# Up-projections of a macaron decoder block by Strassen's scheme over pairs of tiles

## The chip, the cores and the metric

The kernel runs on the eight cores of one Trainium2 chip. Each core works on one of the eight sequences of the batch and exchanges nothing with the others. The metric is the device time in microseconds (us) of the slowest core.

## The reference

One decoder layer in float32 (batch 8, 4096 positions, width 1024, hidden width 2816). Three sub-layers follow one another, each behind an RMS norm that is scaled and shifted by vectors of the conditioning input `c`: a SwiGLU feed-forward network (FFN), a token mixer, and a second FFN. A last norm ends it.

```
mod = silu(c) @ w_mod + b_mod                       # nine vectors of 1024: shifts, scales, gates
h = ada_rmsnorm(x, g_ffn1, sh1, sc1)
gate, up = split(h @ w_in)                          # 1024 -> 2 x 2816
x = x + 0.5 * gt1 * ((silu(gate) * up) @ w_out)     # 2816 -> 1024
proj = ada_rmsnorm(x, g_mix, sh2, sc2) @ w_in_mix   # 1024 -> 2048
x = x + gt2 * concat(conv_group(proj), rglru_group(proj)) @ w_out_mix
... the second FFN with sh3, sc3, gt3, then the final ada_rmsnorm
```

The conv group is a gated unit, a causal depthwise convolution of width 31, a layer norm and a SiLU. The other group is a short convolution of width 4, two sigmoid gates by block-diagonal matrices, and a first-order recurrence along the sequence.

## The kernel before

A sequence is cut into eight tiles of T = 512 positions; a tile is held transposed, features on the partitions, as eight blocks of 128 x 512. All large products are bf16 matmuls of a 128 x 128 weight block with a 128 x 512 block, summed in one of eight PSUM banks (`mms`, L461). The weights come as slabs of 128 x 2048 bf16 (512 KB) into ten SBUF slots.

The first FFN takes tiles 0 to 5 in pairs and tiles 6 and 7 one by one; the second FFN takes all tiles one by one. In an FFN, for each of 22 chunks j of the hidden width (`ffn_in`), one slab holds the gate and up columns of the chunk: per tile eight matmuls make the gate, eight the up half, ACT takes the SiLU of the gate out of PSUM (`act`, L419), DVE multiplies it with the up half in PSUM (`tt`, L441). The down-projection (`ffn_out`) takes 22 matmuls for each of eight output blocks and adds the result to x (`stt`, L437). The float32 weights of the first FFN are cast on their first use by a DMA of the POOL queue and written back to HBM in bf16 by a DMA of the SP queue; later tiles read that copy. `w2o` is treated so too. `win`, `dcw`, `wout` (mixer) and `w2i` (second FFN) are cast from HBM to HBM by the POOL queue while the first FFN runs (`prep`). The conditioning vectors (`mods`, L536) are 88 multiplications of DVE over 128 x 1024 slabs of `w_mod`.

The mixer works on pairs of tiles: `mix_in` per tile (norm, projections, the recurrence), `mix_conv` per pair, `mix_out` per tile; then the tile goes straight on into the second FFN, its x staying in SBUF. All DMAs stand in the queues of SP (plain) and POOL (casts, most stores), all plain DMA issues on L468.

The order of all this isn't the order in the code. `Program.add` records every operation with a duration in a table of the author, a priority and its buffers; `schedule` is a list scheduler, which for each engine takes the next operation by readiness and priority, gives it a buffer of its pool, and so fixes what stands in each engine's queue; slabs are loaded in the order in which their users came out of a first pass. `emit` turns the dependencies into semaphore waits. The engines then run their queues in order. Float32 blocks come from a pool of 40 buffers (`p2`), bf16 blocks from a pool of 62 (`p1`).

## Time and profile before

| what | value |
|---|---|
| runs | 2373.24 us median of 3 (2370.82 to 2373.36) |
| profiled execution, span of its slowest core | 2371.6 us, spans of the eight cores 2357.1 to 2371.6 |
| PE busy | 2258.1 us, 95% of the span |
| DVE, ACT, POOL busy | 1164.3, 1000.2, 197.9 us |
| DMA | 503.88 MB, 212 GB/s in the mean |

The span runs from the first to the last instruction of the core. The page gives no other time of the profiled execution, so the sum of the prediction is made against this span; the median of the runs is 1.6 us above it. PE's busy time counts from the start of a matmul to its modelled end, so the step from one matmul to the next is read from counts over a long window and not from the mean duration. A window's row gives each engine's busy time and count in that stretch.

### The profile page before, as it was taken

The page shows a single profiled execution, that of the slowest core. Times are in us where ns is not written, and L with a number is a line of the kernel's source. Part 1 is how long each engine was busy: PE and PEld are TensorE (multiplying, and loading weights), DVE is VectorE, ACT ScalarE, POOL GpSimd, SP SyncE. Part 2 cuts the span into 40 slices and gives each one's busy share as a digit, 9 for nine tenths or more (in the row PEclk, how much of TensorE's full clock was granted, in tenths as well). Part 3 has the DMA queues.
Part 4 walks back from the last instruction along what each step waited for, and adds up shares of the span by engine and source line. Part 5 has one row for each costly group of instructions (what it writes and reads, how often), then busy time and mean ns, then how long its engine had stood idle before and what let it go on. Part 6 is the DMA issues. An engine that isn't in the chain of part 4 may idle for free.

```text
span 2371.6 us, 34311 instructions; the slowest of 8 cores (2357.1 to 2371.6 us)
## 1 busy us (share of the span) xinstructions
PE 2258.1 (95%) x10692; PEld 1068.2 (45%) x10898; DVE 1164.3 (49%) x1898; ACT 1000.2 (42%) x1445; POOL 197.9 (8%) x374
## 2 busy tenths in 40 slices
PE   2999999999999998999998899999999999999997
PEld 0444444444444453444454344454444454444446
DVE  6325241413143796644685425687426786232423
ACT  2314011401122974304975415886416876231422
POOL 0001100110011003000003001003001003000000
PEclk9999999999999999999999999999999999999998
DMA  9899877797779989999579746667557577455455
GB/s 250 188 258 223 249 227 163 165 188 191 145 178 218 228 225 293 298 290 299 165 202 260 226 158 225 195 209 246 194 165 227 187 237 258 154 191 178 176 188 178
DMA packets 184642, 503.88 MB, mean 212 GB/s; under 512 B 53856, under 2 KB 56032, under 8 KB 183776
## 3 DMA queue, kind: packets, MB, share of 16 engines
q1 hardware_dynamic: 161088, 414.87, 55.2%
q0 software_dynamic: 23376, 86.79, 19.0%
q8 instruction: 92, 1.51, 0.3%
q14 instruction: 86, 0.70, 0.1%
HBM read 482.45 MB, written 88.60 MB: 241 GB/s over the span
## 4 chain that ended last, share of the span: by engine, by line
PE 82%; DMA 6%; DVE 5%; SPq 3%; issue 2%; ACT 1%; DVEq 0%; ACTq 0%; POOLq 0%
PE ps L461 82%; SPq L468 3%; DVE sb_c L437 2%; DMA sb_slab<-w1i 2%; DMA sb_slab<-wmod 1%; DVE sb_c L441 1%; DMA sb_slab<-b_w2i 1%; DMA b_w2o<-sb_slab 1%; DMA sb_slab<-w2o 1%; DVE sb_h L441 1%; ACT sb_c L419 0%; DMA sb_h<-yseq 0%; DVE sb_c L447 0%; ACT L419 0%; DVE sb_c L823 0%
## 5 line engine op out<-in xcount | busy, mean ns | idle before, releaser
L461 PE MATMUL ps<-sb_h,sb_slab 128*128 128x512 bf16 (+1 forms) x9960 | 2172.6, 377 | 63.9 <-ACT sb_h L419 28.2
L461 PEld LDWEIGHTS ps<-sb_h,sb_slab 128*128 128x128 bf16 x10160 | 996.8, 98 | 1222.2 <-issue 77.6
L441 DVE TENSOR_TENSOR sb_h<-ps,sb_c 128x512 bf16<-128x512 f32 x352 | 242.6, 691 | 657.3 <-PE ps L461 558.6
L419 ACT ACTIVATE sb_c<-ps 128x512 f32<-128x512 f32 (+1 forms) x392 | 230.7, 592 | 754.3 <-PE ps L461 731.7
L441 DVE TENSOR_TENSOR sb_c<-sb_c 128x512 f32<-128x512 f32 (+1 forms) x524 | 336.3, 674 | 78.4 <-ACT sb_c L419 73.0
L419 ACT ACTIVATE sb_c<-sb_c 128x512 f32<-128x512 f32 (+1 forms) x324 | 190.2, 610 | 264.5 <-DVE sb_c L437 241.2
L419 ACT ACT_TABLE_LOAD x167 | 214.3, 1283 | 175.2 <-PE ps L461 163.3
L437 DVE SCALAR_TENSOR_TENSOR sb_c<-ps,sb_gth,sb_c 128x512 f32<-128x512 f32 (+1 forms) x136 | 97.8, 719 | 287.1 <-PE ps L461 278.5
L536 DVE SCALAR_TENSOR_TENSOR sb_slab<-sb_slab,sb_crow 128x1024 f32<-128x1024 f32 x88 | 107.4, 1221 | 36.7 <-DMA sb_slab<-wmod 33.5
L419 ACT ACTIVATE sb_h<-sb_c,sb_modv,sb_gs 128x512 bf16<-128x512 f32 x138 | 102.8, 802 | 34.4 <-DVE sb_modv L441 24.1
L905 POOL DMA_DIRECT2D yseq<-sb_h x128 | 67.8, 537 | 154.3 <-ACT sb_h L419 152.5
L468 POOL DMA_DIRECT2D y<-sb_c x56 | 30.5, 546 | 599.0 <-ACT sb_c L419 321.0
L437 DVE SCALAR_TENSOR_TENSOR sb_c<-sb_ux,sb_vecs,sb_c 128x512 f32<-128x512 f32 x96 | 72.1, 751 | 11.1 <-DVE sb_c L437 0.9
L461 PE MATMUL ps<-sb_ub,sb_slab 128*128 128x256 bf16 x576 | 65.7, 273 | 1.5 <-ACT sb_c L419 1.0
L441 DVE TENSOR_TENSOR sb_h<-sb_c 128x512 bf16<-128x512 f32 (+1 forms) x82 | 55.5, 677 | 21.8 <-ACT sb_c L419 16.7
L468 POOL DMA_DIRECT2D xmid<-sb_c x64 | 35.3, 552 | 321.0 <-DVE sb_c L437 315.1
L461 PEld LDWEIGHTS ps<-sb_ub,sb_slab 128*128 128x128 bf16 x576 | 56.0, 98 | 10.8 <-issue 2.2
L437 DVE SCALAR_TENSOR_TENSOR sb_c<-ps,sb_modv,sb_c 128x512 f32<-128x512 f32 x64 | 47.4, 748 | 22.6 <-PE ps L461 18.6
L419 ACT ACTIVATE sb_c<-sb_c,sb_lam 128x512 f32<-128x512 f32 x64 | 50.7, 807 | 1.5
L419 ACT ACTIVATE sb_c<-ps,sb_cst 128x512 f32<-128x512 f32 (+1 forms) x33 | 22.3, 675 | 67.0 <-PE ps L461 64.8
L419 ACT ACTIVATE sb_ux<-ps 128x512 f32<-128x512 f32 x32 | 35.1, 1109 | 28.2 <-PE ps L461 27.6
L461 PE MATMUL ps<-sb_h,sb_ones 128*128 128x512 bf16 (+1 forms) x62 | 23.2, 382 | 24.6 <-DVE sb_h L441 24.6
(56 smaller groups left out, 537.9 us busy)
## 6 DMA issues: line engine op xcount, KB each, us to landing
sb_slab<-b_w2i SPq DMA_DIRECT2D x176, 512.0 KB, 4.0
sb_slab<-b_w2o SPq DMA_DIRECT2D x96, 512.0 KB, 3.6
sb_slab<-wmod SPq DMA_DIRECT2D x88, 512.0 KB, 9.8
sb_slab<-b_w1i SPq DMA_DIRECT2D x88, 512.0 KB, 6.2
sb_c<-xmid SPq DMA_DIRECT2D x128, 256.0 KB, 7.2
sb_slab<-b_win SPq DMA_DIRECT2D x64, 512.0 KB, 4.4
sb_slab<-b_w1o SPq DMA_DIRECT2D x48, 512.0 KB, 6.0
sb_slab<-b_dcw SPq DMA_DIRECT2D x36, 512.0 KB, 4.5
```

Source lines behind the costliest of these rows:

```text
L419: return A("ACT", dur, lambda: (lambda o, i: (lambda h: [h.activation(out=o, in_=i, func=func, bias=bias, scale=scale)]))(out(), in_()), r ...
L437: return A("DVE", dur, lambda: (lambda o, a, b: (lambda h: [h.scalar_tensor_tensor(out=o, in0=a, scalar=scalar, in1=b, op0=op0, op1=op1)]) ...
L441: return A("DVE", dur, lambda: (lambda o, a, b: (lambda h: [h.tensor_tensor(out=o, in0=a, in1=b, op=op)]))(out(), in0(), in1()), reads, wr ...
L461: return [h.matmul(o, lhsT=l, rhs=r, start=(first and i == 0), stop=(last and i == n - 1)) for i, (l, r) in enumerate(pr)]
L468: lambda: (lambda o, i: (lambda h: [h.dma_start(out=o, in_=i)]))(out(), in_()),
L536: return lambda h: [h.scalar_tensor_tensor(out=w, in0=w, scalar=1.0, in1=crow.ap, op0=ALU.mult, op1=ALU.mult, accum_out=o)]
L905: return lambda h: [h.dma_start(out=yc_d[rows[q]:rows[q] + 64, :].rearrange("(g c) n -> c g n", c=32), in_=src[32 * q:32 * q + 32]) for q ...
```

## The change

The up-projection of a chunk for a pair of tiles is a product of a 2 x 2 block matrix of weights (gate and up columns by two halves of the 1024 features) with a 2 x 2 block matrix of activations (two halves of the features by two tiles). The change computes it with seven block products in place of eight, by Winograd's form of Strassen's scheme. A block product is four matmuls of 128 x 512.

- **Weights.** The first pair of each FFN computes plainly (`plain_in`), with slabs cast on use, for `w2i` now too. On each such slab DVE makes four sums of weight blocks in bf16 (`slab_sums`), and SP writes three blocks and the four sums to HBM (`keep_in`), 896 KB for a chunk. The other three pairs read these as two slabs per chunk.
- **Activations.** For a pair DVE makes four sums of blocks of the normed input in bf16 (`hb_sums`).
- **A chunk** (`quick_in`): seven products into three PSUM banks x, y and z. ACT copies three partial results to SBUF, DVE adds three further ones from PSUM to those, ACT takes one SiLU over 128 x 1024, DVE multiplies twice. Bank x is used by four products in turn, each of which adds to what stands there after ACT or DVE has read it.
- **Order.** Both FFNs go by pairs, `ffn(s)` with s = 0 to 3 for the first and 4 to 7 for the second; s = 0 and 4 are plain. The mixers of the pairs 0 to 3 are laid into s = 2, 3, 4 and 5 by the table `MIX`. `mix_out` stores x to HBM, and an FFN loads x twice, for the norm and again for the down-projection. The down-projection stays plain (`QOUT` is off).
- **Memory.** One pool (`gp`, 156 units of 1 KB per partition, a buffer being one, two or four adjoining units) takes the place of `p1` and `p2`; slots for slabs go from ten to eight. Loads and stores of x are of 512 KB. Squares, norm scalings and their sums work on 128 x 1024. The modulation's rows after the first sixteen go through `gp`.
- **Last tile.** Its down-projection isn't split into halves of 256 columns any more.

```diff
-NSLOT = 10
-N_P2 = 40
-N_P1 = 62
+NSLOT = 8
...
+QOUT = False
+NG = 156
...
+MIX = [[(2, 1), (2, 6), (2, 12), (2, 16), (2, 19)],
+       [(3, 1), (3, 6), (3, 12), (3, 16), (3, 19)],
+       [(4, 1), (4, 6), (4, 12), (4, 16), (4, 19)],
+       [(5, 1), (5, 6), (5, 12), (5, 16), (5, 19)]]
...
+        def hb_sums(B, prio):
+            row = lambda i: B[i].q[0].ap.bitcast(BF16)
+            for o, a, b in ((T1, T1, B11), (T2, B22, T1), (T3, T2, B11), (T4, B21, T2)):
+                op = sub16(lambda o=o: row(o), lambda a=a: row(a), lambda b=b: row(b), B[a].q + B[b].q, B[o].q, 4 * T, prio=prio)
+            return op
...
+            sub16(out(0), a21, a22, [slab], [q], n, prio=prio, op=ALU.add, after=after)
+            sub16(out(1), out(0), a11, [slab], [q], n, prio=prio)
+            sub16(out(2), a11, a21, [slab], [q], n, prio=prio)
+            sub16(out(3), a12, out(1), [slab], [q], n, prio=prio)
...
+        def keep_in(nm, j, slab, prio, after=()):
...
+            q = slab_sums(slab, 4, prio, after)
+            wb = dmas("SP", [(d[:, 0:1536], lambda: slab.ap[:, 0:1536])], D_SLAB * 0.75, lambda: wb_sems[slab.slot], [slab], [scr_i[nm][j][0]], prio=prio)
+            dmas("SP", [(d[:, 1536:3584], lambda: q.ap.bitcast(BF16))], D_SLAB, slot_sem(q), [q], [scr_i[nm][j][1]], prio=prio)
...
+            prod(x_, "A11", B11, True, True)
+            copy(ga, x_, dd)
+            prod(z_, "S1", T1, True, True)
+            copy(lambda: c.ap, z_, c)
+            prod(x_, "S2", T2, False, True)
+            copy(gb, x_, dd)
+            prod(y_, "A12", B21, True, True)
+            plus(ga, y_, dd)
+            prod(z_, "S4", B22, False, True)
+            plus(gb, z_, dd)
+            prod(x_, "S3", T3, False, True)
+            plus(lambda: c.ap, x_, c)
+            act(lambda: dd.ap, lambda: dd.ap, AF.Silu, [], [dd], dur=act_us(2 * T), tset=(SILU,), prio=250)
+            last = prod(x_, "A22", T4, False, True)
+            (ha, ha_ap), (hb_, hb_ap) = H[2 * hf][k], H[2 * hf + 1][k]
+            tt(ha_ap, lambda: x_.ap, ga, ALU.mult, [x_, dd], [ha], prio=250)
+            tt(hb_ap, lambda: c.ap, gb, ALU.mult, [c, dd], [hb_], prio=250)
...
+                    slab = cast_slab(wi, j, sync=sync, after=casts[-1:], lat=DMA_LAT if s == 0 and j < 10 else 6.0)
...
+                    op = plain_in(B, H, slab, j, split=(s == 0 and j == 0))
+                    wb = keep_in(wi, j, slab, P.prio + 20, after=(op,) if s == 0 and j < 6 else ())
...
+                    sa = slab_of(w_scr[wi][128 * j:128 * j + 128, 0:2048], scr_i[wi][j], name=f"{wi}{j}a")
+                    sb_ = slab_of(w_scr[wi][128 * j:128 * j + 128, 2048:3584], scr_i[wi][j][1:], cols=1536, name=f"{wi}{j}b")
+                    op = quick_in(B, H, sa, sb_, j, start)
```

How the queues read, at three places. The first is PE in the up-projection of a full FFN step, before (groups of eight matmuls, one bank each, with the semaphores a group waits for) and now, where slab1 holds A11, S1, A12 and A22 of one chunk and slab7 its S2, S3 and S4; slab0 belongs to the chunk before, slab3 to the next.

```order
L461 MATMUL ps<-sb_h,sb_slab 128x512 [waits s_slabSP6,s_dve]
L461 MATMUL ps<-sb_h,sb_slab 128x512 x7
L461 MATMUL ps<-sb_h,sb_slab 128x512 [waits s_dve]
L461 MATMUL ps<-sb_h,sb_slab 128x512 x7
L461 MATMUL ps<-sb_h,sb_slab 128x512 [waits s_dve]
```

```order
L558 MATMUL ps<-sb_gp,sb_slab0 128x512 [waits s_dve]
L558 MATMUL ps<-sb_gp,sb_slab0 128x512 x3
L558 MATMUL ps<-sb_gp,sb_slab7 128x512 [waits s_slabSP7,s_act]
L558 MATMUL ps<-sb_gp,sb_slab7 128x512 x3
L558 MATMUL ps<-sb_gp,sb_slab1 128x512 x4
L558 MATMUL ps<-sb_gp,sb_slab7 128x512 [waits s_act]
L558 MATMUL ps<-sb_gp,sb_slab7 128x512 x3
L558 MATMUL ps<-sb_gp,sb_slab7 128x512 [waits s_act]
L558 MATMUL ps<-sb_gp,sb_slab7 128x512 x3
L558 MATMUL ps<-sb_gp,sb_slab3 128x512 [waits s_slabSP3,s_dve]
```

Before, a group waits for a free bank and a slab; now a group of four waits for ACT or DVE to have read the same chunk's earlier product. Between two products of one chunk that hang on one another stand two other products: A22 of the chunk before behind S1, A12 and S4 behind S2, and A11 and S1 of the next chunk behind S3.

The second place is the queue of POOL around the cast of the second FFN's up weights, before (HBM to HBM, during the first FFN) and now (into slabs, in `ffn(4)`); `useq` and `yseq` are stores of the mixers.

```order
L468 DMA xmid<-sb_c 128x512
L468 DMA b_w2i<-w2i 16x16384
L468 DMA useq<-sb_h 128x512 x4
L468 DMA b_w2i<-w2i 16x16384 x4
L468 DMA useq<-sb_h 128x512 x4
L468 DMA b_w2i<-w2i 16x16384 x2
```

```order
L565 DMA sb_slab<-w2i 128x2048 x5
L565 DMA xmid<-sb_gp 128x1024
L565 DMA sb_slab<-w2i 128x2048 x2
L1193 DMA yseq<-sb_gp 32x2x256 x8
L565 DMA xmid<-sb_gp 128x1024
L1193 DMA yseq<-sb_gp 32x2x256 x24
L565 DMA xmid<-sb_gp 128x1024 x8
L565 DMA sb_slab<-w2i 128x2048
L565 DMA useq<-sb_gp 128x512
L565 DMA sb_slab<-w2i 128x2048
```

Seven of the 22 casts now stand ahead of the mixer's stores of pair 1, the other fifteen behind them. The third place is the queue of SP in the same stretch of the changed kernel: the writing of kept weights (`b_w2i`), between the loads of the mixer.

```order
L573 DMA b_w2i<-sb_slab 128x1536 x3
L565 DMA sb_gp<-xmid 128x1024 x4
L573 DMA b_w2i<-sb_slab 128x1536
L565 DMA sb_slab<-b_wout 128x2048 x2
L573 DMA b_w2i<-sb_gp 128x2048
L565 DMA sb_gp<-xmid 128x1024 x4
L573 DMA b_w2i<-sb_gp 128x2048
```

A write of sums waits for DVE; the loads of `xmid` and `wout` behind it are what `mix_out` needs.

## Rows read from the trace of the kernel before

**Rows 1.** Page, part 1: busy us of each engine (share) and instructions.
```profile
PE 2258.1 (95%) x10692; PEld 1068.2 (45%) x10898; DVE 1164.3 (49%) x1898; ACT 1000.2 (42%) x1445; POOL 197.9 (8%) x374
```

**Rows 2.** Windows, core 0: length; PE, PEld, DVE, ACT, POOL busy; PEclk, DMA share, GB/s.
```profile
0.00:60.00 60.00, 14.37 (x51) 5.85 (x53) 38.23 (x82) 16.96 (x23) 3.54 (x10) 1.00 0.95 250
100.00:700.00 600.00, 597.05 (x2726) 272.00 (x2781) 202.63 (x314) 132.06 (x212) 49.14 (x94) 1.00 0.85 201
780.00:1380.00 600.00, 564.03 (x2661) 267.44 (x2712) 377.25 (x620) 325.53 (x455) 63.27 (x118) 0.97 0.84 247
840.00:900.00 60.00, 59.59 (x348) 34.30 (x352) 55.14 (x96) 45.54 (x68) 2.12 (x5) 1.00 0.86 229
960.00:1080.00 120.00, 119.42 (x546) 54.41 (x556) 67.33 (x114) 21.26 (x33) 4.34 (x8) 1.00 0.90 295
1200.00:1260.00 60.00, 56.58 (x320) 32.15 (x326) 52.08 (x88) 43.21 (x65) 5.84 (x11) 0.97 0.87 217
1260.00:1380.00 120.00, 103.16 (x449) 45.85 (x458) 51.27 (x79) 51.77 (x76) 21.32 (x40) 0.93 0.79 236
1560.00:1620.00 60.00, 57.80 (x337) 33.13 (x340) 52.68 (x87) 46.25 (x76) 0.52 (x1) 1.00 0.74 237
1920.00:1980.00 60.00, 57.66 (x338) 33.12 (x341) 51.17 (x80) 43.08 (x76) 13.18 (x25) 1.00 0.71 237
2316.00:2336.00 20.00, 20.00 (x185) 17.84 (x183) 6.55 (x14) 2.92 (x7) 0.00 (x0) 1.00 0.83 268
2340.00:2372.00 32.00, 15.30 (x139) 13.31 (x137) 12.28 (x32) 11.64 (x25) 0.00 (x0) 0.77 0.30 103
```

**Rows 3.** Groups by line and shape: count | busy us, mean ns | idle before.
```profile
L441 DVE TENSOR_TENSOR sb_c<-sb_c 128x512 f32<-128x512 f32 x500 | 327.2, 686 | 72.1 <-ACT sb_c L419 66.8 <-DVE sb_c L431 0.2 <-DVE sb_c L441 0.2
L441 DVE TENSOR_TENSOR sb_h<-ps,sb_c 128x512 bf16<-128x512 f32 x352 | 242.6, 691 | 657.3 <-PE ps L461 558.6 <-ACT sb_c L419 88.4 <-remote 8.3
L419 ACT ACTIVATE sb_c<-ps 128x512 f32<-128x512 f32 x384 | 228.0, 597 | 743.9 <-PE ps L461 722.0 <-remote 14.0 <-DVE sb_slab L536 6.0
...
L536 DVE SCALAR_TENSOR_TENSOR sb_slab<-sb_slab,sb_crow 128x1024 f32<-128x1024 f32 x88 | 107.4, 1221 | 36.7 <-DMA sb_slab<-wmod 33.5
...
L437 DVE SCALAR_TENSOR_TENSOR sb_c<-ps,sb_gth,sb_c 128x512 f32<-128x512 f32 x120 | 90.0, 750 | 271.1 <-PE ps L461 262.4 <-remote 8.4
...
L419 ACT ACTIVATE sb_crow<-sb_crow 128x1024 f32<-128x1024 f32 x1 | 1.1, 1057 | 0.0
```

**Rows 4.** DMA queues of the whole run, page part 3: packets, MB, share of 16 engines.
```profile
q1 hardware_dynamic: 161088, 414.87, 55.2%
q0 software_dynamic: 23376, 86.79, 19.0%
```

**Rows 5.** DMA of the window 60 to 240 us: queues, then one issue group.
```profile
q0 software_dynamic: 4284, 15.52, 54.1%
q1 hardware_dynamic: 8102, 24.59, 42.2%
...
sb_slab<-b_w1i SPq DMA_DIRECT2D x1, 512.0 KB, 26.8
```

**Rows 6.** Chain that ended last, one piece: start, us, what.
```profile
1304.09 19.23 DMA sb_slab<-b_w2i
```

**Rows 7.** Timeline of the last stretch: start, us, engine, operation, [idle before].
```profile
2355.03 0.48 DVE L437 SCALAR_TENSOR_TENSOR sb_c<-ps,sb_gth,sb_c 128x256 f32<-128x256 f32 x1 [0.81 <-PE ps L461]
2355.60 0.42 ACT L419 ACTIVATE sb_c<-sb_c 128x256 f32<-128x256 f32 x1 [1.99 <-DVE sb_c L437]
2356.19 0.42 DVE L441 TENSOR_TENSOR sb_h<-sb_c 128x256 bf16<-128x256 f32 x1 [0.68 <-ACT sb_c L419]
...
2356.76 0.27 PE L461 MATMUL ps<-sb_h,sb_ones 128*128 128x256 bf16 x1 [1.73 <-DVE sb_h L441]
2357.13 0.47 ACT L419 ACTIVATE sb_c<-ps,sb_cst 128x256 f32<-128x256 f32 x1 [1.11 <-PE ps L461]
...
2361.42 0.41 DVE L427 TENSOR_SCALAR sb_c<-sb_c,sb_gs,sb_modv 128x256 f32<-128x256 f32 x1
```

More of the change, by code:

```diff
@@ L136, in reset, with spots, earliest, take @@
     def reset(self):
-        self.res = [Res() for _ in self.aps]
-        self.free = list(range(self.n))
+        self.res = [Res() for _ in range(self.n)]
+        self.busy = [False] * self.n
+        self.best = {}
+    def spots(self, size):
+        for s in range(0, self.n - size + 1, size):
+            run = range(s, s + size)
+            if not any(self.busy[i] for i in run):
+                yield max(self.res[i].free_t for i in run), s
+    def earliest(self, size):
+        if size not in self.best:
+            self.best[size] = min((t for t, _ in self.spots(size)), default=None)
+        return self.best[size]
+    def take(self, size, now):
+        def cost(spot):
+            t, s = spot
+            quad = range(s - s % 4, min(self.n, s - s % 4 + 4))
+            return (max(t - now, 0.0), -sum(self.busy[i] for i in quad), t, s)
+        _, s = min(self.spots(size), key=cost)
+        for i in range(s, s + size):
+            self.busy[i] = True
+        self.best = {}
+        return s
+    def give(self, s, size):
+        for i in range(s, s + size):
+            self.busy[i] = False
+        self.best = {}
 class VB:
-    def __init__(self, pool=None, ap=None, name=""):
+    def __init__(self, pool=None, ap=None, name="", size=1, spare=0):
         self.pool = pool
@@ L267, in start_of @@
                     continue
-                fr = b.pool.free
-                if not fr:
+                free_t = b.pool.earliest(b.size)
+                if free_t is None or b.pool.n - sum(b.pool.busy) < b.size + b.spare:
                     return None
-                t = max(t, min(b.pool.res[s].free_t for s in fr))
+                t = max(t, free_t)
         return t
@@ L451, in cp, with mms @@
             return A("DVE", dur, lambda: (lambda o, i: (lambda h: [h.tensor_copy(out=o, in_=i)]))(out(), in_()), reads, writes)
-        def mms(bank, pairs, reads, first=True, last=True, cols=512, sub=None, prio=None, after=()):
+        def mms(bank, pairs, reads, first=True, last=True, cols=512, sub=None, prio=None, after=(), more=False):
             n = len(pairs)
@@ L460, in g @@
                 def g(h):
-                    return [h.matmul(o, lhsT=l, rhs=r, start=(first and i == 0), stop=(last and i == n - 1))
+                    return [h.matmul(o, lhsT=l, rhs=r, start=(first and i == 0), stop=(last and i == n - 1), skip_group_check=more)
                             for i, (l, r) in enumerate(pr)]
@@ new lines, in slab_sums @@
+        def slab_sums(slab, nk, prio, after=()):
+            n = 128 * nk
+            q = new(4, "sums")
+            blk = lambda i: (lambda: slab.ap[:, n * i:n * i + n])
+            out = lambda i: (lambda: q.ap.bitcast(BF16)[:, n * i:n * i + n])
+            a11, a12, a22, a21 = (blk(i) for i in range(4))
+            sub16(out(0), a21, a22, [slab], [q], n, prio=prio, op=ALU.add, after=after)
+            sub16(out(1), out(0), a11, [slab], [q], n, prio=prio)
+            sub16(out(2), a11, a21, [slab], [q], n, prio=prio)
+            sub16(out(3), a12, out(1), [slab], [q], n, prio=prio)
+            return q
@@ new lines, in build_program, with mixer @@
+        yrs = {}
+        def mixer(s, ev, pr, gate_op):
+            P.prio = 500 + 100 * s - 40
+            gate_op = (gate_op, ends[s - 1])
+            if ev < 2:
+                yrs[pr, ev] = mix_in(2 * pr + ev, gate_op, P.prio - 5)
+            elif ev == 2:
+                yrs[pr, 2] = mix_conv(pr, gate_op)
+            else:
+                mix_out(2 * pr + ev - 3, yrs[pr, ev - 3], gate_op)
+            if s in out_x:
+                for o in out_x[s][XG:]:
+                    o.after.append(P.last)
@@ L996, in emit_cb @@
             fn = (op.fn if op.on == op.eng else op.alt[2])()
[L997 to L998 removed]
+            rs = [r for b in op.reads for r in b.res]
+            ws = [r for b in op.writes for r in b.res]
             e = engs[op.on]
```

806 lines of the change are left out of this document (483 added, 323 removed).

## The prediction

> **What bounds the kernel now.** The busy times say PE: 2258.1 of 2371.6 us, with DVE and ACT at half and less [rows 1]. The windows say how [rows 2]. From 100 to 700 us PE loads 2781 weight blocks in 600 us, 0.2158 us for a 512-column matmul, at full clock (PEclk 1.00); only fewer matmuls shorten such a stretch. In 2316 to 2336 it is 20 us for 183 to 185 matmuls of 256 columns, 0.1087 us each. The built program has 9934 of 512 and 964 of 256 columns, so 2143.8 + 104.8 = 2248.6 us of matmuls; the other 10 us of PE's busy time are stretches at half clock and ends of chains.
>
> PE is idle for 113.5 us: 45.6 before the first products (60 less 14.37), 16.7 behind the last (32 less 15.30), 36.0 between 780 and 1380, 15 elsewhere [rows 2]. Part of the middle is DMA: the chain of waits has a load of `b_w2i` there that took 19.2 us [rows 6], and 1260 to 1380 lost 16.8 us [rows 2], where the twelve casts of `w2o` stand. Where DVE is densest, 51 to 55 us of 60, PE idles for 0.4, 3.4, 2.2 and 2.3 us, in the mean 2.1 us in 60 [rows 2].
>
> **The matmuls removed.** Three pairs in each of two FFNs have 22 chunks: 132 chunks, each with 28 matmuls for 32, 528 less. The last tile's 352 halves become 176 whole ones. The new program has 9584 and 608: 2068.2 + 66.1 = 2134.3 us. All of it lies on the path, as PE is the bound: **-114.3 us**. The rest of the sum asks how much of that is given back.
>
> **The chain inside a chunk.** PE needs 28 x 0.2158 = 6.04 us for a chunk, DVE 5 x 0.691 = 3.46, ACT 3 x 0.597 + 1.057 = 2.85 [rows 3]. What is new is that PE waits for readers of its own results. The hops are in the last stretch [rows 7]: PE to ACT 0.10 (2356.76 + 0.27 to 2357.13), DVE to ACT 0.09, ACT to DVE 0.17, DVE to PE 0.15. A result stands 0.16 us after the next matmul can start (0.27 for 256 columns against a step of 0.11). Behind A11 the copy takes 0.16 + 0.10 + 0.60 + 0.15 = 1.01 us, and two other products (1.73 us) stand between, as the order shows: 0.7 us to spare. S2 to S3 has the same; S3 to A22, over DVE, takes 0.16 + 0.10 + 0.69 + 0.15 = 1.10, with 0.6 to spare. So a step without mixer (s = 1, 6, 7) should run without gaps; I take 2 us each for s = 6 and 7.
>
> **DVE in the mixer steps.** PE's time in such a step is 968 matmuls of the FFN and 400 whole and 160 half ones of the mixer, 208.9 + 86.3 + 17.4 = 312 us. DVE's 1164.3 us [rows 1] less modulation (107.4), the FFN's multiplications (242.6) and its adds (90.0) [rows 3] leave 724 us for mixers and 24 norms of tiles: 181 us a pair, and 162 without the final norm (2 x 14 x 0.686). So s = 2 and 3 have 22 x 3.46 + 16 x 0.75 + 24 x 1.22 (modulation) + 162 + the four sums of activations. These, and the 176 sums of weights in s = 0 and 4, are bf16 with bf16, which no row here shows. From the float rows (512 elements 0.686, 1024 elements 1.221) 2048 would take 0.686 + 3 x 0.535 = 2.29 us as the upper end; half of it is the lower. I take the upper, as the nearest rows are two-tensor operations too. Then DVE has 289 us of 312, 93%, for whole steps; s = 5, without modulation but with a final norm, 89%; s = 4, with 60 us of weight sums, 284 of 332. Those are the shares of today's densest windows, so I take their 2.1 us in 60: 11 us each in s = 2 and 3, 9 in s = 5. The Trainium skill, "VectorE: DVE Perf Modes", section on the perf-mode tier table, says that a `tensor_tensor` of 16-bit operands in SBUF runs at twice the float rate, 1224 ns for 2048 elements; by it s = 2 falls to 284 us and the sum by less than 1 us.
>
> **DMA.** The plain queue took 55.2% of 2371.6 us for 414.87 MB, 3.16 us a MB [rows 4]. With many casts, from 60 to 240, POOL's queue took 54.1% of 180 us for 15.52 MB, 6.27 us a MB [rows 5]. Each chunk now reads 0.92 MB where a pair read 0.52, x moves more often, and kept weights add 20.2 MB of writes to each plain step. By step, from the sizes in the program, MB of casts and of the rest: s = 0, 17.3 and 47.5, 259 us in 273; s = 1, 11.0 and 47.0, 217 in 209; s = 2 and 3, 85.3 plain, 270 in 312; s = 4, 17.3 and 72.7, 338 in 332; s = 5, 230 in 312; s = 6 and 7, 122 in 209. So s = 1 and s = 4 ask for a little more than there is. For a cover speaks that 295 GB/s (960 to 1080) left PE 119.4 of 120 us [rows 2], and that eight slots, four chunks of two slabs, are 24 us of lead; against it, that a load of `b_w1i` among the casts landed after 26.8 us [rows 5]. I take 5 us for s = 0, 10 for s = 1, and 20 for s = 4, where POOL's queue holds fifteen casts behind the mixer's stores, and SP's holds `mix_out`'s loads behind writes that wait for DVE. The ends: nothing at all (first rival), and all of the excess (second).
>
> **Start and end.** The first slabs, the modulation and the first tile's norm are the same work; 0, between -2 and +5 (two slots fewer). At the end the last block of x goes through wider operations: add 0.75, square 1.06, add 1.22, two of 0.69, two of ACT's 0.6, four scalings of 1.22, one last of 0.6, with PE and the hops some 12.5 us from the last product, where about 7 passed before (just ahead of 2355.03, to 2361.42 + 0.41) [rows 7]. The last store is of 512 KB in place of 128, 2 us more at the rate above with its landing. **+8 us**, at least 3 (scalings beside other work), at most 12.
>
> **The sum.** Idle inside the run: 5 + 10 + 11 + 11 + 20 + 9 + 4 = 70 us against 113.5 - 45.6 - 16.7 = 51.2, so +18.8. 2371.6 - 114.3 + 18.8 + 8 = 2284.1 us of span; the median of the runs shown is 1.6 above the span, so **2286 us**. 0.2% of the time, 4.7 us, is about what a measurement of this kernel can tell from no change.
>
> **Rivals.** *All cover holds* (14%): the planner spreads DMA better than my rows, the stalls of 780 to 1380 go, DVE's gaps are filled with other products. Inside idle is 15 us: 2371.6 - 114.3 - 36 + 8 + 1.6 = 2231; with half of that gain 2249.
>
> *DMA becomes the bound* (17%): each of 21 casts in s = 1 and 34 in s = 4 costs what each of the twelve of `w2o` cost, 16.8 / 12 = 1.4 us [rows 2], 29 and 48 us. Inside idle is 5 + 29 + 22 + 48 + 9 + 4 = 117: 2371.6 - 114.3 + 66 + 8 + 1.6 = 2333, and up to 2346 with half clock behind the stalls (PEclk below 1 in that window). For it speaks the 26.8 us landing; against it, that both queues fill 96% of 60 to 240 us [rows 5] with PE at work. The Trainium skill, "DMA: Bandwidth & Descriptors", section on queues, rings and completion order, says that each DMA engine takes the queues it has work for in turn, packet by packet, so that slab loads get no precedence over casts; by that rule this rival is what s = 1 and 4 do, and the landing of 26.8 us agrees.
>
> *The chain inside a chunk costs more than the product it saves* (10%, the other side): ACT or DVE takes a mixer's or a norm's operation ahead of a copy, and PE stands. It decides from (114.3 - 8 - 18.8) / 132 = 0.66 us a chunk, the spare time of one hop. With one 1.22 us operation ahead on two hops of each chunk, 2 x (1.22 - 0.6) = 1.24 us, 164 us in all: 2450. Against it: without a mixer both engines are half free.
>
> *No change* (4%): the prices just cancel, 2369 to 2378. That the matmuls aren't removed is excluded by the counts of the built programs.
>
> **Chances and range.** The forecast's own range, 2262 to 2310 by the bounds above, has 55%. Faster by over 0.2%: 55 + 14 + 17 = 86%; same 4%; slower 10%. The range 2238 to 2346 leaves out half of the first rival and the last two, some 20%.
>
> **What would show it.** Right: weight loads at 0.2158 us through s = 1, 6 and 7; in s = 2, 3 and 5 idle PE of 2 us in 60, released by DVE and ACT; DVE near 70% of the span; the idle of s = 1 and 4 released by slabs. Wrong: PE released by ACT's copies or DVE's adds all through s = 6 and 7 (third rival); tens of us behind slabs in s = 1 or 4 (second); full clock lost over long stretches.

## The result and the profile after

| | before | after |
|---|---|---|
| median | 2372.03 us of 4 runs | 2345.48 us of 4 runs (2343.05 to 2350.86) |
| after to before | | 0.9895, 95% interval 0.9879 to 0.9911 |
| profiled execution, slowest core | span 2371.6 us | span 2349.3 us (core 2), time 2350.86 us |

The change makes the kernel 1.05% faster; 3.6% was forecast, and 2345 us stands at the upper end of the range. Executions in which a whole die ran slower, or that took over 1.5% more than the kernel's fastest, are left out of every ratio and interval.

Page, part 1, of the changed kernel; it answers to [rows 1].

```profile
PE 2175.2 (93%) x10192; PEld 997.4 (42%) x10192; DVE 1487.4 (63%) x2277; ACT 1189.6 (51%) x1602; POOL 181.1 (8%) x342
```

PE has the 10192 matmuls that were counted. The next rows are the windows of the changed kernel, core 2, one for each step (columns as in [rows 2]). A step goes from its first product to that of the next one; the built program says how many products stand between. The first row is the start, the last one what lies behind the last matmul.

```profile
0.00:48.90 48.90, 1.17 (x2) 0.22 (x3) 34.08 (x75) 12.39 (x15) 2.70 (x8) 1.00 0.93 267
48.90:312.10 263.20, 239.25 (x1062) 105.33 (x1063) 115.89 (x199) 67.32 (x90) 19.61 (x37) 0.97 0.90 222
312.10:566.60 254.50, 220.19 (x973) 95.79 (x972) 126.22 (x182) 86.20 (x117) 14.82 (x29) 0.94 0.97 227
566.60:864.60 298.00, 289.58 (x1401) 136.41 (x1400) 230.61 (x357) 197.68 (x265) 9.18 (x17) 0.99 0.78 243
864.60:1191.40 326.80, 318.11 (x1529) 148.46 (x1528) 246.59 (x387) 201.66 (x278) 33.79 (x63) 0.99 0.84 257
1191.40:1545.20 353.80, 340.42 (x1620) 159.01 (x1619) 225.56 (x368) 191.36 (x251) 40.75 (x76) 0.98 0.91 251
1545.20:1868.00 322.80, 314.07 (x1516) 147.67 (x1515) 238.52 (x344) 222.52 (x297) 32.38 (x60) 1.00 0.70 222
1868.00:2112.90 244.90, 241.29 (x1124) 109.28 (x1123) 150.88 (x208) 113.29 (x162) 23.50 (x44) 1.00 0.66 215
2112.90:2331.60 218.70, 210.54 (x975) 95.14 (x973) 113.46 (x156) 91.29 (x124) 4.35 (x8) 0.99 0.46 152
2331.60:2349.30 17.70, 0.58 (x1) 0.07 (x1) 5.56 (x6) 5.87 (x8) 0.00 (x0) 0.50 0.39 157
```

Take from a step's length its matmuls at the full rate (0.2158 us, 0.1087 for half ones), and what is left is its **loss**. For s = 0 that is 263.2 - 1062 x 0.2158 = 34.0 us; the other steps follow in the same way (s = 2, 3 and 4 have 152 half matmuls each, s = 5 has 135, s = 6 has 17).

| step | forecast | measured loss, core 2 |
|---|---|---|
| s = 0 | 5 | 34 |
| s = 1 | 10 | 44.5 |
| s = 2, 3 | 11 each | 12, 13 |
| s = 4 | 20 | 20.5 |
| s = 5 | 9 | 10 |
| s = 6, 7 | 2 each | 4, 0 up to its last product |

Six steps lost about as much as was forecast. Two didn't, by 29 and 34.5 us, and that is nearly all of the miss: 2349.3 against 2284.1 us of span. The other cores show the same (s = 0 29.5 to 36.9, s = 1 38.2 to 44.8 on the six cores whose matmul records are complete). Of the two losses 24.0 and 34.3 us are idle PE (lengths less busy times); the forecast's 5 and 10 are idle time too. The other 10 us of each are matmuls slower than the full rate (busy times less the full-rate times), at a granted clock of 0.97 and 0.94 in the mean of the step.

Where PE stood, from the timeline of PE in s = 0 and 1 (start, us, operation, [idle before and releaser]):

```profile
87.02 31.93 PE L558 MATMUL ps<-sb_gp,sb_slab 128*128 128x512 bf16 x136 [7.19 <-ACT sb_gp L516]
...
194.08 8.87 PE L558 MATMUL ps<-sb_gp,sb_slab 128*128 128x512 bf16 x32 [6.61 <-DVE sb_gp L538]
207.40 37.24 PE L558 MATMUL ps<-sb_gp,sb_slab 128*128 128x512 bf16 x164 [4.45 <-DVE sb_gp L538]
...
395.32 20.16 PE L558 MATMUL ps<-sb_gp,sb_slab 128*128 128x512 bf16 x84 [8.93 <-DMA sb_slab<-b_w1i]
...
450.19 4.49 PE L558 MATMUL ps<-sb_gp,sb_slab 128*128 128x512 bf16 x12 [5.71 <-DMA sb_slab<-b_w1i]
462.51 5.15 PE L558 MATMUL ps<-sb_gp,sb_slab 128*128 128x512 bf16 x12 [7.83 <-DMA sb_slab<-b_w1i]
```

In s = 0 the first wait is for the second tile's norm. The next two are named after DVE, and DVE's own timeline says why DVE was late:

```profile
192.10 1.23 DVE L653 SCALAR_TENSOR_TENSOR sb_gp<-sb_gp 128x1024 f32<-128x1024 f32 x1 [11.46 <-DMA sb_gp<-wmod]
205.42 1.23 DVE L653 SCALAR_TENSOR_TENSOR sb_gp<-sb_gp 128x1024 f32<-128x1024 f32 x1 [10.89 <-DMA sb_gp<-wmod]
```

Two rows of the modulation stood at the head of DVE's queue before their loads had landed, and the chunks' operations behind them waited too. In s = 1 the waits are slabs of kept weights. The DMA view of 360 to 480 us has the reason (queues, then an issue group with KB and median landing):

```profile
q1 hardware_dynamic: 5717, 19.25, 56.9%
q0 software_dynamic: 414, 6.82, 42.2%
...
sb_slab<-b_w1i SPq DMA_DIRECT2D x11, 512.0 KB, 22.3
```

99% of the engines' time is taken: 42.2% by POOL's queue, nearly all of it casts, at 0.422 x 120 / 6.82 = 7.4 us a MB, and 56.9% by SP's. A slab of kept weights takes 22.3 us to land (median). Ahead of that s = 0 has a hole. The windows of 60 to 120 us, and POOL's next cast:

```profile
60.00:80.00 20.00, 19.82 (x92) 8.82 (x90) 9.98 (x18) 10.34 (x13) 1.06 (x2) 1.00 0.75 168
80.00:100.00 20.00, 12.98 (x49) 5.43 (x50) 11.18 (x23) 8.11 (x12) 0.53 (x1) 0.83 0.23 59
100.00:120.00 20.00, 18.95 (x88) 8.42 (x86) 10.14 (x24) 3.58 (x6) 1.59 (x3) 1.00 1.03 223
```

```profile
95.99 0.53 POOL L565 DMA_DIRECT2D sb_slab<-w1i  x1 [29.07 <-DVE sb_gp L538]
```

All eight slots are held until the second tile's norm is there, so the casts pause for 29 us and DMA runs at 23%; from 100 to 280 us it is full.

### The profile page after: what moved, and what is told of

The parts are those of the page before. It is cut to its first block, busy times and chain, and to the rows that moved or that the text cites. A ratio compares the mean times of both kernels' runs of the same rounds, so it can differ in the third digit from the quotient of the medians.

```text
span 2349.3 us, 34252 instructions; the slowest of 8 cores (2328.6 to 2349.3 us)
## 1 busy us (share of the span) xinstructions
PE 2175.2 (93%) x10192; PEld 997.4 (42%) x10192; DVE 1487.4 (63%) x2277; ACT 1189.6 (51%) x1602; POOL 181.1 (8%) x342
## 4 chain that ended last, share of the span: by engine, by line
PE 75%; DMA 12%; DVE 3%; ACT 3%; SPq 3%; issue 3%; DVEq 0%; ACTq 0%; POOLq 0%
PE ps L558 75%; DMA sb_slab<-b_w1i 3%; ACT sb_gp L516 2%; DVE sb_gp L538 2%; SPq L565 2%; DMA sb_gp<-x 2%; DMA b_w1i<-sb_slab 1%; DMA sb_gp<-wmod 1%; DMA sb_slab<-b_wout 1%; DMA sb_slab<-w1i 1%; DMA sb_slab<-b_dcw 1%; DMA sb_gp<-xmid 1%; SPq L573 1%; ACT L516 1%; DMA sb_slab<-wmod 1%
## 5 line engine op out<-in xcount | busy, mean ns | idle before, releaser
L558 PE MATMUL ps<-sb_gp,sb_slab 128*128 128x512 bf16 x9456 | 2090.1, 382 | 105.9 <-DVE sb_gp L538 27.6
L558 PEld LDWEIGHTS ps<-sb_gp,sb_slab 128*128 128x128 bf16 x9456 | 926.9, 98 | 1246.4 <-issue 165.2
L538 DVE TENSOR_TENSOR sb_gp<-ps,sb_gp 128x512 f32<-128x512 f32 (+1 forms) x616 | 419.9, 689 | 296.6 <-PE ps L558 181.5
L538 DVE TENSOR_TENSOR sb_gp<-sb_gp 128x512 bf16<-128x512 f32 (+3 forms) x596 | 518.7, 894 | 120.5 <-ACT sb_gp L516 109.7
L516 ACT ACTIVATE sb_gp<-ps 128x512 f32<-128x512 f32 (+1 forms) x556 | 321.3, 589 | 526.3 <-PE ps L558 496.5
L516 ACT ACTIVATE sb_gp<-sb_gp 128x1024 f32<-128x1024 f32 (+2 forms) x342 | 314.7, 927 | 355.4 <-DVE sb_gp L538 149.3
L534 DVE SCALAR_TENSOR_TENSOR sb_gp<-ps,sb_gth,sb_gp 128x512 f32<-128x512 f32 x128 | 95.6, 748 | 180.8 <-PE ps L558 179.2
L516 ACT ACTIVATE sb_gp<-sb_gp,sb_modv,sb_gs 128x512 bf16<-128x512 f32 (+1 forms) x203 | 157.6, 807 | 64.9 <-DVE sb_gp L538 37.2
L653 DVE SCALAR_TENSOR_TENSOR sb_gp<-sb_gp 128x1024 f32<-128x1024 f32 x72 | 87.6, 1216 | 35.7 <-DMA sb_gp<-wmod 35.6
L534 DVE SCALAR_TENSOR_TENSOR sb_gp<-sb_ux,sb_vecs,sb_gp 128x512 f32<-128x512 f32 x96 | 72.1, 751 | 9.6
L538 DVE TENSOR_TENSOR sb_gp<-sb_slab 128x512 bf16<-128x512 bf16 x88 | 36.9, 421 | 27.3 <-DMA sb_slab<-w1i 23.3
```

What stands on the lines that cost most here:

```text
L516: return A("ACT", dur, lambda: (lambda o, i: (lambda h: [h.activation(out=o, in_=i, func=func, bias=bias, scale=scale)]))(out(), in_()), r ...
L534: return A("DVE", dur, lambda: (lambda o, a, b: (lambda h: [h.scalar_tensor_tensor(out=o, in0=a, scalar=scalar, in1=b, op0=op0, op1=op1)]) ...
L538: return A("DVE", dur, lambda: (lambda o, a, b: (lambda h: [h.tensor_tensor(out=o, in0=a, in1=b, op=op)]))(out(), in0(), in1()), reads, wr ...
L558: return [h.matmul(o, lhsT=l, rhs=r, start=(first and i == 0), stop=(last and i == n - 1), skip_group_check=more) for i, (l, r) in enumera ...
L653: return lambda h: [h.scalar_tensor_tensor(out=a, in0=a, scalar=1.0, in1=c, op0=ALU.mult, op1=ALU.mult, accum_out=o)]
```

## The experiments

Losses are worked out as above, on the cores with complete records, and ranges are over those cores. Where one pair of cores ran at a granted clock of 0.81 in a step (last section), that pair is left out of that step. In the changed kernel s = 0 lost 33 us in the mean of the cores. All diffs are against the changed kernel unless it says otherwise; as the planner orders the whole program anew for each edit, steps that an edit doesn't name can change too.

**Second tile's x early.**

```diff
-                        wait_for(x1_loads[j // 2], casts[max(0, j - 3)])
+                        wait_for(x1_loads[j // 2], casts[0])
```

> The loads of the second tile's x in s = 0 wait only for the first cast. In the changed kernel s = 0 takes 263 us for 229 us of matmuls (34 lost) and s = 1 takes 254 us for 210 (45 lost). Theory of order (eight slots, all held until the second tile's norm is there, and casts that stop meanwhile): the pause of POOL's casts from 66 to 96 us shrinks to about 15 us, s = 0 loses 15 us or less, the time falls by about 20 us. Theory of bytes (DMA is full, whatever the order): only the idle DMA time of 75 to 96 us can come back, s = 0 loses 20 to 30 us, s = 1 still about 45, the time falls by 5 to 12 us. Theory of the chain inside a chunk: no change.

s = 0 lost 17.8 to 31.2 us (mean 25), s = 1 36.3 to 42.2; ratio to before 0.9895 (0.9819 to 0.9971), that of the changed kernel. Some 8 us came back in s = 0, which is what the theory of bytes gave. The theory of order wasn't put to a full test: the pause of the casts fell to 21 us and not to 15 (POOL, core 7).

```profile
85.56 0.53 POOL L565 DMA_DIRECT2D sb_slab<-w1i  x1 [21.18 <-DVE sb_gp L538]
```

**Fewer bytes in s = 0.** `keep_in` returns for `w1i` behind one write; the later steps read columns 0 to 1536 for the second slab. The return stands behind `slab_sums`, so DVE still makes the sums (116.20 us and 200 operations in s = 0 on core 5, where the changed kernel's core 2 has 115.89 and 199): only the writing is left out, not the computing.

```diff
+            if nm == "w1i":
+                return dmas("SP", [(d[:, 0:2048], lambda: slab.ap[:, 0:2048])], D_SLAB, lambda: wb_sems[slab.slot], [slab], scr_i[nm][j], prio=prio)
```

> The writing of the sums of w1i and their computing in s = 0 are left out: SP writes one block of 128 x 2048 for a chunk in place of 128 x 1536 and 128 x 2048, 8.65 MB less, and the later steps read as many bytes as now, plain blocks in the place of sums. Theory of bytes: at 3.28 us a MB of the plain queue (46.6% of 180 us for 25.59 MB) 28 us of DMA go, s = 0 loses about 8 us in place of 34, s = 1 still about 45; the time falls by about 25 us. Theory of order: the slots come free at the same points, s = 0 loses at least 25 us. Theory of the chain: no change in s = 0 either, as it is plain.

s = 0 lost 24.2 to 30.5 us (mean 27); ratio 0.9865 (0.9806 to 0.9924). 8.65 MB were worth 6 us and not 28: bytes alone don't make this loss.

**No preparing casts.**

```diff
-            jobs = [(a, q) for a in batch if isinstance(a, int) for q in range(8)] + [j for j in prep if j[0] in batch]
+            jobs = [(a, q) for a in batch if isinstance(a, int) for q in range(8)]
...
-            return slab_of(dr(w_scr[nm], r), [scr[nm][r]], prio=prio, after=after, name=f"{nm}{r}")
+            return slab_of(dr(w_scr["w1i"], r)[:, 0:2048], scr_i["w1i"][r], prio=prio, after=after, name=f"{nm}{r}")
```

> The 21 casts of win, dcw and wout in s = 1 are left out, and the mixers read kept blocks of w1i in their place, as many bytes. Theory of bytes: 11 MB at 7.4 us a MB (42.2% of 120 us for 6.82 MB), some 80 us of DMA, are gone from s = 1, which then loses under 12 us in place of 45; s = 0 as before at 34; the time falls by 35 us or more. Theory of order (x loads and slabs stand in one queue, gated by the planner): s = 1 still loses 25 us or more. Theory of the chain inside a chunk: s = 1 still loses about 40 us, as its chunks are the same.

This kernel leaves out the mixers' weights and reads other blocks in their place. The window of s = 1, core 5 of this run:

```profile
309.60:519.30 209.70, 209.70 (x973) 95.06 (x972) 126.24 (x182) 85.27 (x117) 4.25 (x8) 1.00 0.68 225
```

PE is busy for 209.70 of 209.70 us. The whole loss of s = 1 goes with 21 casts (0 to 0.9 us on four cores), so each cost 2 us in the mean, and the chunks of Strassen's scheme run without a gap when their slabs are there. s = 0 kept 32.0 to 35.9. Ratio 0.9714 (0.9638 to 0.9790).

**The first FFN plain.**

```diff
+            if nm == "w1i":
+                return dmas("SP", [(d[:, 0:2048], lambda: slab.ap[:, 0:2048])], D_SLAB, lambda: wb_sems[slab.slot], [slab], scr_i[nm][j], prio=prio)
...
+                elif not second:
+                    slab = slab_of(w_scr[wi][128 * j:128 * j + 128, 0:2048], scr_i[wi][j], name=f"{wi}{j}a")
+                    op = plain_in(B, H, slab, j, split=False)
```

> The first FFN computes plainly in all four pairs, with its plain weights kept (512 KB written and read a chunk); Strassen's scheme is left in the second FFN. 264 matmuls come back, 57 us. Theory of bytes: s = 0 loses about 8 us in place of 34 and s = 1 about 20 us of 229 in place of 45 of 210, so that 2349 + 57 - 26 - 25 or about 2350 us come out: the scheme in the first FFN brings next to nothing. Theory of order: s = 0 and 1 lose as much as now, and the time is 2349 + 57 = 2406 us. Theory of the chain: s = 1 loses nothing, s = 0 as now, 2349 + 57 - 45 = 2361.

The windows of s = 0 and 1, core 5:

```profile
47.40:305.40 258.00, 238.44 (x1062) 105.51 (x1063) 77.46 (x108) 66.10 (x89) 19.57 (x37) 0.96 0.79 194
305.40:556.50 251.10, 232.94 (x1061) 104.51 (x1060) 78.79 (x113) 50.81 (x72) 14.78 (x29) 0.96 0.81 197
```

The slowest core had a span of 2395.6 us, so the scheme in the first FFN is worth some 46 us of its 57. None of the three expectations (2350, 2406 and 2361 us) is met; that of order is nearest. In s = 1 the scheme brings nothing: with 88 matmuls more this step takes 240 to 254 us (mean 246), where it takes 248 to 254.5 (mean 251) with the scheme. There DMA is busy for 97% of it, here for 81%. The gain comes from s = 2 and 3: 685.9 us together here (core 5), 624.8 with the scheme (core 2), though part of that is mixers' work which the plan laid into another step. And s = 0, without any sums, still lost 25.0 to 28.9.

**The casts of dcw one step later.**

```diff
-        LATE = {1: [M_SC2, M_SH2, "win", "dcw", "wout"], 2: [M_GT2, M_SC3, M_SH3], 3: [M_GT3, M_SCF, M_SHF]}
+        LATE = {1: [M_SC2, M_SH2, "win", "wout"], 2: [M_GT2, "dcw", M_SC3, M_SH3], 3: [M_GT3, M_SCF, M_SHF]}
```

> The nine casts of dcw stand in s = 2, behind the rows for the gate, in place of s = 1; all else as in the changed kernel. Theory of bytes: at 512 KB each and 7.4 us a MB (42.2% of 120 us for 6.82 MB) some 35 us of DMA leave s = 1, which loses about 10 us in place of 38 to 45; in s = 2, with a load of 85 MB in 300 us, they find room, so that it loses 12 to 25 us where it lost 13. The time falls by 20 to 35 us. If what counts is that any casts stand there (each blocks the plain loads behind it), s = 1 still loses 12 / 21 of its 45, about 25 us, and s = 2 loses 20 us more: the time stays.

s = 1 lost 12.4 to 15.2 us, s = 2 14.8 to 17.8. Nine casts fewer gave 28 us, three a cast; in s = 2, with DMA at 78% before, they cost 4. It is the amount in a step that is already full that counts, not that casts stand there. The four cores without such a stretch had spans of 2301 to 2320 us; the slowest, with a clock of 0.81 in s = 1 and 2, 2350.9.

**x early and fewer bytes.** Both edits.

> Both edits of the first two runs: x of the second tile early, and 8.65 MB fewer written in s = 0 (the sums of w1i left out, plain blocks read in their place). Alone they left 18 to 45 us (five of six cores with full records between 25 and 45) and 24 to 30 us of loss in s = 0, where the changed kernel has 30 to 37. Theory that a backlog decides (casts pause at 66 us while all slots are held, and behind that DMA is full for 120 us whatever is written): s = 0 loses 10 to 18 us, less than with either edit, as the pause and the bytes behind it both shrink. Theory that the turn of a slot decides (write landing and cast landing, some 40 us for eight slots): 20 us or more stay.

s = 0 lost 18.1 to 27.0 us (mean 23, against 25 and 27 with one edit alone); ratio 0.9876 (0.9854 to 0.9897). Four of six cores are at the 20 us or more of the second theory, two below; the next run tests that theory by itself.

**Nine slots.**

```diff
-NSLOT = 8
+NSLOT = 9
-NG = 156
+NG = 152
```

> Nine slots for slabs in place of eight, with the pool of buffers cut from 156 to 152 units. Theory that the turn of a slot decides in s = 0: with a ninth more slabs under way s = 0 loses 20 us or less in place of 30 to 37. Theory of bytes: s = 0 loses about as much as before, between 28 and 37, as the same bytes pass; s = 1 loses 38 to 45 as before. The later steps are ordered anew by the planner with the smaller pool and are not compared.

s = 0 lost 28.3 to 36.0 us, so the number of slots isn't it. s = 1 lost 35.2 to 36.0, a little less than the 38 to 45 expected. The whole kernel was slower than before, 1.0042 (1.0024 to 1.0060); nine slots and the smaller pool aren't told apart there.

**Three edits of order.** Those of the first run and of the dcw casts, and

```diff
-                mods(M_GT1, ins[12:20])
+                mods(M_GT1, ins[2:18:2])
```

> Three edits of order alone: dcw's casts in s = 2, the x of the second tile early, and the eight rows of the first FFN's gate spread over chunks 2 to 16 in place of 12 to 19. Theory of bytes in their steps: s = 1 loses about 10 us in place of 38 to 45 and s = 0 about 25 in place of 33; the time is 2345 - 30 - 8 or about 2305 us, below both kernels. Theory that order gives nothing back (bytes moved only shift the loss): 2340 us or more.

s = 0 lost 20.5 to 32.8 us, s = 1 10.8 to 13.5; 0.9810 (0.9737 to 0.9883). The losses are those of the first theory. Its 2305 us weren't reached: the runs took 2313, 2321, 2345 and 2349 us, and in the last two one pair of cores had a lower mean clock than the others (0.97 against 0.98).

**The gate's rows further behind their loads.**

```diff
-                    prio=P.prio, after=() if slab else (afters[q],) + tuple(paced[-2:-1]), lat=DMA_LAT if slab else 6.0)
+                    prio=P.prio, after=() if slab else (afters[q],) + tuple(paced[-7:-6] if rows else paced[-2:-1]), lat=DMA_LAT if slab else 6.0)
...
-                last = A("DVE", 1.22, f, [crow], [b, modr[m]], after=(afters[q],), prio=P.prio if slab else 260)
+                last = A("DVE", 1.22, f, [crow], [b, modr[m]], after=((rows or afters)[q],), prio=P.prio if slab else 260)
...
-                mods(M_GT1, ins[12:20])
+                mods(M_GT1, ins[8:16], rows=ins[13:21])
```

> The eight rows for the gate of the first FFN: each load is placed four chunks earlier, each multiplication on DVE one chunk later, so that five chunks (34 us) lie between where two lay before; all else, and all bytes, as in the changed kernel. Theory of the blocked queue: DVE takes its operations in order, and in the changed kernel stands 26 us in s = 0 at rows whose loads land after 31 us; PE then stands behind it for 6.6 and 4.5 us and runs at half clock for 10 us behind that. Without these waits s = 0 loses 18 to 24 us in place of 30 to 37, and DVE waits under 5 us for wmod. Theory of bytes alone: the same loss, 30 to 37 us, with PE standing for slabs in place of DVE.

s = 0 lost 20.6 to 29.2 us, some 7 less, yet the whole gained next to nothing: 0.9893 (0.9867 to 0.9919), where the changed kernel on the same chip had 0.9885. The steps behind s = 1, up to the last matmul, lost 66 to 77 us there and 58 to 70 in the changed kernel. The waits of DVE went only in part; its row for `wmod` from 60 to 312 us, core 0 (waits in total, times, longest):

```profile
DVE sb_gp L653 <- DMA sb_gp<-wmod: 24.3, 5, 11.6
```

Five chunks, 34 us, lay between in the plan, but the eight loads, issued by SP between its writes of kept weights, took 27 to 39 us to land on this core.

**All that gave something, together.** The edits of the first run, of the dcw casts and of the run before, and for the last tile

```diff
+                        if end:
+                            tt(o, o, lambda: r_.ap, ALU.mult, [r_], [b], prio=310)
...
+                            q = "PL" if e else "SP"
+                            dma(q, lambda d=d: d.ap, o, D_CHUNK, slot_sem(b, q), [b], [d])
```

> All edits of order that gave time back, together: dcw's casts in s = 2, the second tile's x early, the gate's rows as in the run before, and for the last tile scaling and stores by halves of 512 columns over the queues of SP and POOL. By sums of the single effects on cores that aren't slowed: s = 0 loses about 15 us in place of 33, s = 1 about 12 in place of 41, s = 2 2 us more, the tail is 3 us shorter: 2345 - 18 - 29 + 2 - 3 or about 2297 us. If the edits only shift one loss to the next step, 2320 us or more.

s = 0 lost 15.4 to 26.7 us (mean 21, expected 15), s = 1 12.0 to 14.9, as expected; 0.9834 (0.9779 to 0.9889). Three runs took 2312 to 2315 us, three 2341 to 2345, where about 2297 was expected; in each of the latter three one pair of cores had a lower mean clock, as in the last two of the run of three edits. The tail grew from 17.7 to 21.8 us behind the last matmul, against the expectation: the scaling of a block's second half waited for the store of its first half, since the program tracks whole buffers.

```profile
2292.87 2.85 DVE L538 TENSOR_TENSOR sb_gp<-sb_gp 128x512 f32<-128x512 f32 x4 [0.67 <-DMA y<-sb_gp]
```

**The changed kernel again**, on the same chip.

> The changed kernel, once more, on the chip of the two runs before, for comparison: 2343 to 2351 us if nothing but the program sets its time; if one pair of cores is slowed in the steps that are full of DMA, s = 0 and s = 1 lose over 10 us more each on that pair and the time is up to 2360 us.

2344.06 us (2340.28 to 2347.57), 0.9885 (0.9871 to 0.9899); s = 0 lost 31.5 to 36.0, s = 1 38.0 to 41.8. That is the first case of the expectation; no pair had a lower clock.

**Rows still earlier, x spread in s = 1, the tail mended.** Against the run before last:

```diff
-                mods(M_GT1, ins[8:16], rows=ins[13:21])
+                mods(M_GT1, ins[4:12], rows=ins[13:21])
...
-                xs = [load_x(src, t, prio=P.prio - 50, after=(ins[15 + 2 * i],) * 4, lat=6.0, spare=16) for i, t in enumerate(tiles)]
+                xs = [load_x(src, t, prio=P.prio - 50, after=tuple(ins[min(21, 11 + 1 * (4 * i + f))] for f in range(4)) if s == 1 else (ins[15 + 2 * i],) * 4, lat=6.0, spare=16) for i, t in enumerate(tiles)]
```

> The run e10 with three edits more: the loads of the gate's rows stand eight to nine chunks ahead of their multiplications (e10: five); in s = 1 the eight loads of x for the down-projection are spread over chunks 11 to 18 in place of two bursts of four at chunks 15 and 17; the last tile is scaled by halves, with both halves ahead of the stores, which are whole again. Theory of the blocked queues: in e10 DVE still stood 10 us at a late row (PE 7.7 us behind it), and in s = 1 a slab that stood behind bursts of x in SP's queue landed after 24 us (PE 8.1 us). Both waits go: s = 0 loses 8 to 15 us in place of 15 to 27, s = 1 3 to 8 in place of 12 to 15; the tail is 15 to 17 us in place of 21.8 (a scaling waited for a store of the same buffer there). In all 2328 - 20 or about 2308 us by the median, about 2290 where no pair of cores is slowed. Theory of bytes: the same bytes in the same steps, s = 0 and 1 lose as in e10; 2322 us by the tail alone.

0.9805 (0.9791 to 0.9819); the runs in it took 2319 to 2326 us, where about 2308 was expected. s = 0 still lost 15.8 to 27.2 us, s = 1 8.4 to 17.8, and the steps behind s = 1 lost 70 to 82 us where the run of all edits together lost 60 to 70. On core 3 DVE no longer waits for `wmod` in s = 0, and this is what stands where the row stood:

```profile
199.07 20.02 PE L558 MATMUL ps<-sb_gp,sb_slab 128*128 128x512 bf16 x92 [2.94 <-ACT sb_gp L516]
227.10 1.19 PE L558 MATMUL ps<-sb_gp,sb_ones 128*128 128x512 bf16 x2 [8.01 <-DVE sb_gp L538]
```

`sb_ones` is the norm of the next pair, whose x came late. The tail was 18.7 us, against 15 to 17 expected and 17.7 in the changed kernel: scaling by halves brought nothing.

**Order and bytes apart.** The next two have one order for s = 0 (x of the second tile, rows and next x all early) and differ there in the 8.65 MB. To the edits of the first run and of the rows comes

```diff
-                    xn = load_x(src, tiles[t2], prio=400 + 100 * s, after=(gate[t2],) * 4, lat=6.0)
+                    xn = load_x(src, tiles[t2], prio=400 + 100 * s, after=((prev_i[14] if s == 1 and t2 == 0 else gate[t2]),) * 4, lat=25.0 if s == 1 else 6.0)
```

> The second tile's x early, the gate's rows loaded eight to nine chunks ahead, x for the next pair's norm at chunk 14 of s = 0 in place of 18 and priced by the planner at 25 us to land in place of 6, and 8.65 MB fewer written in s = 0 (the sums of w1i left out, plain blocks read in their place). Theory of bytes: with 28 us of DMA less and no late load in a queue s = 0 loses 5 to 12 us (changed kernel 30 to 37, e6 with x early and fewer bytes 18 to 27). Theory of order: the same 5 to 12 us. If neither holds, 16 us or more stay.

> The same three edits of order in s = 0 with all bytes of the changed kernel, dcw's casts in s = 2, the last tile scaled by halves. Theory of bytes: DMA stays full from 90 us to the end of s = 0 and what is late changes again: s = 0 loses 16 to 25 us, as in e10 and e12 (15 to 27). Theory of order: 5 to 12 us, and a time about 8 us below e12's 2324.5.

s = 0, first with fewer bytes (core 3), then with all of them (core 4):

```profile
47.80:288.00 240.20, 234.68 (x1062) 104.92 (x1063) 114.64 (x198) 67.92 (x91) 19.56 (x37) 0.99 0.86 207
```

```profile
47.50:295.20 247.70, 235.25 (x1062) 104.54 (x1063) 116.31 (x201) 65.13 (x88) 19.55 (x37) 0.99 0.96 235
```

With fewer bytes the loss was 7.7 to 18.0 us (mean of six cores 14), with all 18.5 to 30.1 (mean 23), against 33 in the changed kernel. The first lies between its expectations (5 to 12, or 16 and more), the second is what the theory of bytes gave for it. So the three edits of order make some 10 us of the loss, bytes some 9 once the order is mended (6 if it isn't), and 14 stay, most of them ahead of 130 us, around the second tile's norm and the backlog behind it; what these hang on wasn't tried further and stays open. The second of the two took 0.9756 of before (0.9725 to 0.9788); the runs in it took 2313, 2314 and 2322 us. That it is faster than the run of all edits together, with its three runs of 2312 to 2315 us, isn't shown.

## Why the prediction was wrong

- **Matmuls removed, -114.3 us.** Right. 10192 matmuls ran, and steps without DMA trouble took 0.2158 us for each: s = 7 up to its last product, and s = 1 without casts, have no loss.
- **The chain inside a chunk.** Right: s = 1 without casts has no gap, and the third rival is out. Where a slab came late and a chunk stood alone in PE's queue, the hops did show: waits of 0.94 to 1.17 us, six times in s = 1.
- **DVE in the mixer steps, 11, 11 and 9 us.** The sizes came out, 12, 13 and 10, but by luck: DVE was to be busy for 93, 93 and 89% of these steps and was for 77, 75 and 74%. PE's waits of s = 3 (us in total, times, longest) were mostly for slabs; ACT and DVE released nearly all of them in s = 2 and 5.

```profile
PE ps L558 <- DMA sb_slab<-b_dcw: 3.4, 3, 1.3
PE ps L558 <- DVE sb_gp L653: 2.3, 1, 2.3
PE ps L558 <- DMA sb_slab<-b_w1i: 1.4, 2, 1.2
```

  The upper end that was taken for the bf16 sums was far too high:

```profile
L538 DVE TENSOR_TENSOR sb_gp<-sb_slab 128x512 bf16<-128x512 bf16 x88 | 36.9, 421 | 27.3 <-DMA sb_slab<-w1i 23.3
...
L538 DVE TENSOR_TENSOR sb_gp<-sb_gp 128x2048 bf16<-128x2048 bf16 x24 | 28.9, 1221 | 2.4 <-ACT sb_gp L516 1.6
```

  421 and 1221 ns stand where 686 and 2290 were taken. The rule of the Trainium skill ("VectorE: DVE Perf Modes", perf-mode tier table) that gives 1224 ns agrees with this trace.
- **DMA, "5 us for s = 0, 10 for s = 1, and 20 for s = 4".** This step failed, in its first two values: 24.0 and 34.3 us of idle PE, and 10 us each of slower matmuls behind it, for which the sum had no term (only the second rival had one). For s = 1 the bytes were weighed rightly, 57.9 MB against 58.0, but a MB was priced too low. DMA was busy for 97% of 254.5 us, 247, where 217 were forecast for 209 of matmuls; so some 37 us were over and not 8. The queues of s = 1, core 2:

```profile
q1 hardware_dynamic: 12570, 42.47, 58.1%
q0 software_dynamic: 1824, 15.21, 38.4%
```

  SP's queue (q1) took 3.48 us a MB there, where 3.16 was taken from the mean of a whole run [rows 4]; without the casts it took 3.10 in this step (42.73 MB in 63.1% of 209.7 us). POOL's queue (q0) took 97.7 us, where 69 for its casts and 13 for its stores were in the sum. How much of a busy engine's time is one queue holding up the other isn't shown. The 21 casts were worth 42 us in all (second rival: 29, 1.4 each; measured 2 to 3).

  s = 0 was not forecast as a place of loss, since its 259 us of DMA were set against 273 us that include the start, when DMA was full already (93% of the first 48.9 us). The step behind the start had 90% of 263.2 us, 237, for 229 of matmuls, and nobody asked what holds the slots until the second tile's norm, so that DMA stands at 23% meanwhile.

  s = 4, with more casts than s = 1, lost what was forecast, but not for the reasons given: its longest wait is for a load of the mixer.

```profile
1246.96 51.21 PE L558 MATMUL ps<-sb_gp,sb_slab 128*128 128x512 bf16 x224 [6.58 <-DMA sb_gp<-yseq]
```

- **Which rival it was.** The second, "DMA becomes the bound" (2333 to 2346), for s = 1; its 48 us for s = 4 did not come, and 34 us in s = 0 did. The Trainium skill ("DMA: Bandwidth & Descriptors", queues, rings and completion order) says that a DMA engine takes the queues it has work for in turn. The traces agree with it: slabs land after 22.3 us beside the casts of s = 1 and after 3.6 us in the same window without them. Fewer bytes alone would shorten landings too; the two weren't told apart.
- **Start and tail.** PE began at 48.9 us, 4 later than before and inside the bounds. Behind the last product of the down-projection (2319.66 + 3.19, first row below; the second is the last scaling) 26.5 us pass, where about 16.6 did: 10 more, 8 forecast, 3 to 12 the bounds.

```profile
2319.66 3.19 PE L558 MATMUL ps<-sb_gp,sb_slab 128*128 128x512 bf16 x14
...
2339.44 0.81 ACT L516 ACTIVATE sb_gp<-sb_gp,sb_modv,sb_gs 128x512 f32<-128x512 f32 x1 [0.50 <-DVE sb_gp L524]
```

- **The range and the chances.** The median is inside by half a microsecond, which is luck: one of the four runs, 2350.86 us, lies outside. A range whose upper end is the second rival needed that rival's bytes in s = 0 as well.
